# An expert's further passes moved between its base gate/up and down products

## The reference, cut to what matters

```python
logits = (t @ router_w + router_b)           # t: (256, 1024), 32 experts
top_val, top_idx = lax.top_k(logits, 4)      # each token goes to 4 experts
gates = jax.nn.softmax(top_val, axis=-1)
# for every expert e, over the tokens that chose it:
gu = xe @ w_gu[e] + b_gu[e]                  # (n_e, 1024) @ (1024, 2048)
g, u = jnp.split(gu, 2, axis=-1)
g = jnp.minimum(g, 7.0); u = jnp.clip(u, -7.0, 7.0)
act = (u + 1.0) * (g * jax.nn.sigmoid(1.702 * g))
y = (act @ w_down[e] + b_down[e]) * gate     # (n_e, 1024) @ (1024, 1024), summed per token
```

## Time and profile before

| | |
|---|---|
| median of 3 runs | 1359.74 us (1357.9 to 1360.75) |
| the profiled execution: time / span | 1358.61 / 1356.6 us |
| PE, PEld busy | 1284.8 us (95%), 591.3 us (44%) |
| DVE, ACT, POOL busy | 491.4, 187.3, 15.7 us |
| read from memory | 476.1 MB, 352 GB/s over the span |
| chain that ended last | PE 73%, DMA 21%, DVE 3%, issue 2% |

### The profile page before, as it was taken

One profiled execution on the slowest core, in us unless ns is written; L12 is line 12 of the kernel. 1 busy time (PEld: TensorE's weight loads), 2 busy tenths in 40 slices (PEclk: granted clock), 3 DMA queues, 4 the chain that ended last, 5 costly groups with the idle time before them and its releaser, 6 DMA issues.

```text
span 1356.6 us, 16429 instructions
## 1 busy us (share of the span) xinstructions
PE 1284.8 (95%) x5992; PEld 591.3 (44%) x5993; DVE 491.4 (36%) x1030; ACT 187.3 (14%) x377; POOL 15.7 (1%) x48
## 2 busy tenths in 40 slices
PE   4999999999998999999999999999999986999997
PEld 3866866778752333333333333333333321333332
DVE  3032665331143333333333333333333332333334
ACT  2101323332021001000110000110001000001101
POOL 0000000110000000000000000000000000000000
PEclk9999999999999999999999999999999998999999
DMA  9858674326678999999999999999999999399995
GB/s 356 308 186 296 222 241 170 125 73 263 237 289 315 409 428 430 427 430 428 428 429 426 431 427 430 390 427 428 428 429 429 427 430 428 132 431 426 429 428 212
DMA packets 59183, 477.55 MB, mean 352 GB/s; under 512 B 4991, under 2 KB 5076, under 8 KB 32532
## 3 DMA queue, kind: packets, MB, share of 16 engines
q1 hardware_dynamic: 58852, 476.11, 85.6%
q10 hardware_dynamic: 304, 1.06, 0.2%
HBM read 476.10 MB, written 1.05 MB: 352 GB/s over the span
## 4 chain that ended last, share of the span: by engine, by line
PE 73%; DMA 21%; DVE 3%; issue 2%; SPq 0%; ACT 0%; DVEq 0%; ACTq 0%
PE bank L1577 23%; DMA down_ring<-in_w_down 15%; PE bank L1613 14%; PE bank L1260 10%; DMA gu_ring<-in_w_gu 6%; PE bank L1406 4%; PE bank L1253 4%; PE bank L1566 3%; PE bank L1544 3%; PE bank L1308 2%; PE bank L1469 2%; PE bank L1536 1%; PE bank L1367 1%; DVE scratch L1085 1%; DVE scratch L1083 1%
## 5 line engine op out<-in xcount | busy, mean ns | idle before, releaser
L1577 PE MATMUL bank<-gu_ring,scratch 128*64 128x512 f32 x2048 | 464.3, 600 | 12.6 <-issue 7.3
L1577 PEld LDWEIGHTS bank<-gu_ring,scratch 128*64 128x64 f32 x2048 | 143.9, 138 | 299.8 <-issue 292.7
L1613 PE MATMUL bank<-down_ring,scratch 128*64 128x512 f32 x1024 | 233.8, 598 | 18.4 <-DMA down_ring<-in_w_down 13.8
L1260 PE MATMUL bank<-gu_ring 128*128 128x256 f32 x640 | 143.8, 381 | 0.0
L1613 PEld LDWEIGHTS bank<-down_ring,scratch 128*64 128x64 f32 x1024 | 70.1, 136 | 139.2 <-issue 128.9
L1260 PEld LDWEIGHTS bank<-gu_ring 128*128 128x128 f32 x640 | 119.8, 190 | 18.6 <-issue 1.3
L687 ACT ACTIVATE scratch<-bank 128x512 f32<-128x512 f32 x32 | 19.1, 597 | 692.1 <-PE bank L1577 692.1
L1073 DVE TENSOR_TENSOR scratch<-bank,bgu 128x512 f32<-128x512 f32 x32 | 22.2, 692 | 254.5 <-PE bank L1544 254.5
L1055 DVE TENSOR_TENSOR xres<-xres,bank 128x512 f32<-128x512 f32 x132 | 81.8, 682 | 40.1 <-PE bank L1566 40.1
L1544 PEld LDWEIGHTS bank<-ident,scratch 128*128 128x128 f32 x392 | 41.1, 140 | 79.5 <-ACT scratch L687 26.0
L1536 PE MATMUL bank<-xn,onehot 128*64 128x512 f32 x264 | 69.6, 605 | 0.0
(11 more groups left out here) (265 smaller groups left out, 793.3 us busy)
## 6 DMA issues: line engine op xcount, KB each, us to landing
gu_ring<-in_w_gu SPq DMA_DIRECT2D x128, 2048.0 KB, 23.8
down_ring<-in_w_down SPq DMA_DIRECT2D x64, 2048.0 KB, 17.4
gu_ring<-in_w_in SPq DMA_DIRECT2D x32, 1024.0 KB, 7.8
gu_ring<-in_w_ada SPq DMA_DIRECT2D x16, 1024.0 KB, 7.0
down_ring<-in_w_ada SPq DMA_DIRECT2D x8, 512.0 KB, 10.6
gu_ring<-in_w_ada SPq DMA_DIRECT2D x8, 512.0 KB, 11.6
gu_ring<-in_w_pa SPq DMA_DIRECT2D x4, 1024.0 KB, 6.3
gu_ring<-in_w_pb SPq DMA_DIRECT2D x4, 1024.0 KB, 6.3
```

Source lines behind the costliest of these rows:

```text
L1260: last = M(dst[:, b * T:(b + 1) * T], group_chunk(group, kt // 4)[:, kt % 4, cols], hT[:, kt, :], start=kt == 0, stop=kt == KT - 1)
L1577: last = M(bank[f // 2][64 * a:64 * a + 64, :], xT[:, kt % 4, kt // 4, :], gu_ring[:, 8 * half + kt, f * 512:(f + 1) * 512], start=kt == 0 ...
L1613: last = M(bank[7][64 * a:64 * a + 64, :], act_sb[:, kt % 4, kt // 4, :], down_ring[:, kt // 2, (kt % 2) * D + a * 512:(kt % 2) * D + (a + ...
```

## The change

`further_passes` is called in the midst of the expert: on PE behind `way_back` and ahead of base down, on ACT behind `copy_back`, on DVE between the last `act_ready` and `take(item + 1)`. Only the load of the count stays at the expert's head. For this a pass gets small areas of its own: its picks (`f_pick`, `f_gates`), the columns of `u_raw` behind `f_back` (`f_x`), the unused half of `g_sb` (`f_act_sb`), and it gives back through banks 0 to 3 instead of 4 to 7. The picks of an expert's first pass are made for every expert, early in DVE's work (`further_pick`), and those of the next pass in the pass ahead of it. The loop of six turns becomes two by three. PE no longer waits at a pass's end for DVE's adds, nor in a pass for `slot_in`. SP loads from `passes` how many passes stand ahead and waits for `f_gu_done` before it refills a half of the ring.

```diff
-        def further_passes(eng, expert, one_pass):
-            count = eng.value_load(passes[0:1, 0, bass.ds(expert, 1)], min_val=0, max_val=FURTHER_BLOCKS)
+        def further_count(eng, expert):
+            return eng.value_load(passes[0:1, 0, bass.ds(expert, 1)], min_val=0, max_val=FURTHER_BLOCKS)
+        def further_passes(eng, expert, count, one_pass):
             with eng.If(count > 0):
                 before_it = eng.value_load(passes[0:1, 1, bass.ds(expert, 1)], min_val=0, max_val=T * TOPK // FCAP)
-                with eng.Fori(0, FURTHER_BLOCKS) as b:
-                    with eng.If(count > b):
-                        one_pass(b, before_it + b)
+                with eng.Fori(0, 2) as part:
+                    with eng.If(count > part * (FURTHER_BLOCKS // 2)):
+                        with eng.Fori(0, FURTHER_BLOCKS // 2) as n:
+                            b = part * (FURTHER_BLOCKS // 2) + n
+                            with eng.If(count > b):
+                                one_pass(b, before_it + b)
...
             def load_item_gu(item, half):
+                passes_made = sp.value_load(passes[0:1, 2, bass.ds(item - 1, 1)], min_val=1, max_val=T * TOPK // FCAP + 1)
                 for j in range(4):
                     sp.wait_ge(gu_used, item * 8 + (2 * j - 14))
+                    if j == 0:
+                        sp.wait_ge(f_gu_done, passes_made)
...
-            V.tensor_copy(passes[:], passes_f[:]).then_inc(passes_ready, 1)
+            V.tensor_scalar(passes[:, 2, :], passes_f[:, 1, :], 1.0, None, ALU.add)
+            V.tensor_copy(passes[:, 0:2, :], passes_f[:]).then_inc(passes_ready, 1)
...
+            def further_pick(expert, first, made):
+                for tt in range(TT):
+                    V.tensor_scalar(f_pick[:, tt, :], iota[:, 0:FCAP], first,
+                                    r1[:, tt, bass.ds(expert, 1)], ALU.add, ALU.is_equal).then_inc(f_onehot, 1)
+                dve.wait_ge(f_onehot, made * 2 + 2)
+                for tt in range(TT):
+                    V.tensor_scalar(f_gates[:, tt, :, :].rearrange("p a (k s) -> p (a k) s", k=2),
+                                    f_pick[:, tt, :].unsqueeze(1).to_broadcast([P, 4, FCAP]),
+                                    gates[:, tt, bass.ds(expert, 1)], None, ALU.mult).then_inc(f_gated, 1)
...
             def expert(item, half, fills):
+                count = further_count(pe, item)
...
                 way_back(item)
+                further_passes(pe, item, count, lambda b, k: further(item, half, fills, k))
                 for kt in range(KT):
...
             def further(expert, half, fills, k):
-                pe.wait_ge(xTe_ready, expert + 1)
-                pe.wait_ge(back_ready, expert + 1)
-                pe.wait_ge(f_onehot, k * 2 + 2)
+                pe.wait_ge(xraw_ready, expert + 2)
+                pe.wait_ge(f_onehot, (expert + k) * 2 + 2)
...
-                    M(bank[4 + n][:, :], f_back[rows_, tt * P:(tt + 1) * P], f_y[rows_, :], start=True, stop=True
+                    M(bank[n][:, :], f_back[rows_, tt * P:(tt + 1) * P], f_y[rows_, :], start=True, stop=True
                       ).then_inc(f_given, 1)
-                pe.wait_ge(f_added, k * 4 + 4)
-                nc.tensor.transpose(bank[2][:, 0:P], ident[:], ident[:])
```

More of the change, by code:

```diff
@@ L455, in load_item_down @@
                     load_down(item, a)
+            sp.wait_ge(passes_ready, 1)
             load_item_gu(2, 0)
@@ L685, in expert @@
             def expert(item):
+                count = further_count(act, item)
                 act.wait_ge(g_done, item + 1)
@@ L693, in expert @@
                 copy_back(item)
+                further_passes(act, item, count, further)
             def further(b, k):
                 act.wait_ge(f_taken, k + 1)
-                A(in_blocks(x_raw[:, 0:2 * P]), bank[4][:, 0:2 * P].rearrange("s (p r) -> s r p", r=2), ACT.Copy).then_inc(f_xraw, 1)
+                A(in_blocks(f_x), bank[4][:, 0:2 * P].rearrange("s (p r) -> s r p", r=2), ACT.Copy).then_inc(f_xraw, 1)
                 act.wait_ge(f_back_done, k + 1)
                 A(f_back, bank[5][:, 0:T], ACT.Copy).then_inc(f_back_ready, 1)
-                act.wait_ge(f_gu_done, k + 1)
+                act.wait_ge(f_gu_done, k + 2)
                 A(in_blocks(g_raw), by_fours(bank[0][:, :]), ACT.Copy).then_inc(f_raw, 1)
@@ L1004, in _ @@
             dve.wait_ge(counts_done, 1)
-            own.then(V.tensor_scalar(over[:, 0:FURTHER_BLOCKS], pass_start[0:NE, :], bank[0][0:NE, 0:1], None, ALU.is_lt))
+            own.then(V.tensor_scalar(over[:, 0:FURTHER_BLOCKS], pass_start[0:NE, 0:FURTHER_BLOCKS], bank[0][0:NE, 0:1], None, ALU.is_lt))
             V.tensor_reduce(over[:, FURTHER_BLOCKS:FURTHER_BLOCKS + 1], over[:, 0:FURTHER_BLOCKS], AX.X, ALU.add
@@ L1070, in expert @@
                 add_given(item - 1)
+                count = further_count(dve, item)
+                before_it = dve.value_load(passes[0:1, 1, bass.ds(item, 1)], min_val=0, max_val=T * TOPK // FCAP)
+                further_pick(item, pass_start[:, 0:1], item + before_it)
                 dve.wait_ge(gT_done, item + 1)
@@ L1086, in expert @@
                                            ).then_inc(act_ready, 1)
+                further_passes(dve, item, count, lambda b, k: further(item, b, k))
                 take(item + 1)
@@ L1110, in further @@
                 g, u, sg = g_sb[:, :, :, 0:FCAP], u_sb[:, :, :, 0:FCAP], sig[:, :, :, 0:FCAP]
[L1111 to L1119, removed]
+                dve.wait_ge(act_ready, expert * 2 + 2)
                 dve.wait_ge(f_takenT, k + 1)
@@ L1146, in _ @@
             V.memset(small[:, 7:8], 0.0).then_inc(f_mark, 1)
+            V.memset(small[:, 6:7], 0.0).then_inc(f_gu_done, 1)
             with dve.Fori(0, NE) as n:
                 own.start_at(n * PER + start)
-                further_passes(dve, n, lambda b, k: further(n, b, k))
                 expert(n)
@@ L1656, in further @@
                         row = 64 * a + FCAP * (kt % 2)
[L1657 removed]
+                        last = M(bank[7][row:row + FCAP, :], f_act_sb[:, kt % 4, kt // 4, :],
                                  down_ring[:, kt // 2, (kt % 2) * D + a * 512:(kt % 2) * D + (a + 1) * 512],
@@ L1689, in _ @@
                 for half in range(2):
-                    further_passes(pe, n * 2 + half, lambda b, k: further(n * 2 + half, half, n + 1, k))
                     expert(n * 2 + half, half, n + 1)
```

30 lines of the change are left out of this document (16 added, 14 removed).

## The result

| | before | after |
|---|---|---|
| median (range, runs) | 1359.18 us (1357.9 to 1360.75, 4) | 1343.41 us (1342.69 to 1343.86, 4) |
| ratio, 95% interval | | 0.9882 (0.9861 to 0.9903) |
| profiled execution: time / span | 1358.61 / 1356.6 us | 1342.69 / 1340.7 us |
| PE, DVE busy | 1284.8, 491.4 us | 1277.4, 518.2 us |

The kernel is faster by 15.8 us, in the profiled pair by 15.9.

What follows compares the result with a forecast made beforehand. Transfers were taken to bound the experts ahead of the pass (29.37 us), PE those behind (27.37). The sum -11.2 + 0.2 + 0.3 = -10.7 took the profiled 1358.61 to 1347.9 us; median forecast 1349.0, range 1346 to 1352.

Steps and rivals of the forecast that it cites:

- branches in: PE's entry into the pass, a load, three branches and two loop heads: 0.9 us, ends 0.3 and 2.0.
- take to gate/up: Take, copy, transposes and scaling at the pass's start: 3.6 us against 4.1 at half clock, ends 3.2 and 4.1.
- down: The pass's 32 down records on PE, clock partly falling: 5.2 us, ends 3.7 and 6.4.
- result, give back, branches out: End of the pass on PE: 2.6 us for result and give back, 1.5 for branches out.
- the pass: The further pass of expert 25, all exposed in its new place: 25.0 us against 36.2, so -11.2.
- the one-for-one way to the end: Behind the pass PE alone sets the six following experts, so the pass's gain reaches the end undiminished.
- The start: First loop border, where PE stalled 3.49 us: stall may change by -3.5 to +3.5, taken as +0.3.
- The wait for the picks: PE's wait for DVE's picks in the old pass, counted as 2.99 us of the 36.17 the pass adds.
- What every expert pays: PE's branch ahead of base down, DVE's four picks and SP's load, in every expert: 0.
- The first: Deeper gain, clock at its upper level through the pass, branches hidden: -14, 1345.5 us and less; chance 0.10.
- third: Transfers take back what is won: no change, 1359 to 1361 us; chance 0.05.
- The fourth: Slower, the branch in the midst of every expert isn't hidden: 1374 us at 1.5 us each; chance 0.08.

Runs made afterwards that it cites:

- e12: The changed kernel again with no edit, on the same chip as e9 to e11: 1344.08 us, ratio 0.9882.
- e1: The changed kernel with the loop of six turns again in place of two by three: 1346.89 us, ratio 0.9924.
- e2: The changed kernel with every pass's picks made at the head of the pass again, none ahead: 1348.92 us, ratio 0.9933.
- e9: The kernel of e5 with the picks made late, at the head of the pass: 1352.12 us, ratio 0.9943.
- e5: The changed kernel with passes at the expert's head, keeping early picks, small areas, two by three turns, no wait for adds: 1351.94 us, ratio 0.9945.
- e7: The changed kernel with every expert's count of further passes set to 0: 1332.27 us, ratio 0.981.
- e8: The kernel before with every expert's count of further passes set to 0: 1336.67 us, ratio 0.9842.
- e10: The changed kernel with 640 never-reached matmuls behind each pass body on PE, always jumped over: 1651.67 us, ratio 1.2149.
- e11: The changed kernel with 192 never-reached matmuls behind each pass body on PE, always jumped over: 1660.65 us, ratio 1.2215.
- e3: The kernel of e2 with PE also waiting for the pass's adds and a last transpose at the pass's end: 1355.25 us, ratio 0.9972.
- e4: The kernel of e3 with passes back at the expert's head and PE's waits for weights inside the pass: 1357.53 us, ratio 0.9997.
- e6: The kernel before with unused identity products (6, 8, 6 and 8) on PE ahead of the pass's waits: 1359.12 us, ratio 0.9987.

## Why the prediction fell short

The steps, in the order of the prediction, in the profiled pair:

| term, us | predicted | low end | measured |
|---|---|---|---|
| branches in | 0.9 | 0.3 | 0.24 |
| take to gate/up | 3.6 | 3.2 | 3.14 |
| gate/up | 7.15 | | 7.13 |
| middle up to down | 4.04 | | 3.93 |
| down | 5.2 | 3.7 | 3.70 |
| result, give back, branches out | 4.1 | 3.1 | 3.69 |
| the pass | 25.0 | 21.5 | 21.83 |
| ahead of the loop's expert 24 | +0.5 | | -1.6 |

(The pass: 1157.32 less 1106.12, less the period of 29.37.)

- **What bounds, the 29.37 and 27.37 us, one pass at expert 25, the one-for-one way to the end:** right, the periods and the way to the end to 0.1 us.
- **The pass, 3.2 us too long. The failed step is the down product**, "I take 5.2": half of that miss. I let the clock fall because PE stands still about 4 us ahead of it. It does so in some executions (4.96 in e12, 5.06 in e1) and not in others (3.64 in after, and in e2 with the same wait of 2.62). Branches in (0.7 us), the take (0.5) and the way out (0.4) make up the rest. The first two came out just below their low ends (0.24 against 0.3, 3.14 against 3.2): I had bounded the take by the slow old pass, and behind 0.43 us of idle time its 16 records ran at full clock (1.07 us against 1.93), as in e1 and e12. The down product alone did not put the time below the range: in e12 it took 4.96 us, near my 5.2, and that execution took 1344.49 us.
- **The start, 2.1 us off, the largest single term.** This step failed too. I put +0.3 on the stall at the loop's first border (it might double, move or vanish) and +0.2 on DVE's extra instruction. The stall vanished. Of the 1.6 us won there, 1.2 lie ahead of the mixture of experts, in work that the change doesn't touch, and differ between any two executions; 0.4 lie behind, where the mean over the variants is 2.4. Most of the vanished stall is taken back by the transfers later, which the sum should have said: a stall ahead of experts that wait for transfers is not paid one for one. Why the old place fetches at the first border and the new one shows nothing at its jumps isn't settled.
- **The wait for the picks.** I named 2.99 us of "PE's wait for the picks" as part of what the pass cost. The sum didn't use it, but the reason was wrong: e9 against e5 shows that such a wait costs at most 0.6 us there. What made the old pass dear is what came behind the landing at 1128.85: branches that waited for the adds, the clock, and the whole base gate/up.
- **What every expert pays, 0:** right (0.19 us as before, and e7 is not slower than e8). That e7 is 4.4 us faster by the medians is a gain outside the pass that the prediction had no term for and no run explains.
- **The rivals.** The first, "the clock stays at its upper level through the pass, the branches hide", is what the profile shows; I gave it 0.10, against 0.59 for the forecast. The transfers took nothing back (third). The fourth did not occur and would have at a longer jump (e10, e11).

**Where the 16 us come from**, taken apart from the changed kernel by the medians: late picks cost 5.5, the wait for the adds 6.3 more, the old place 2.3 more (not clear of noise, and not in the profiles); six turns by themselves 3.5, of which the profile shows 1.2. Taken away alone, the place costs 8.5. The parts don't add, since in the old place early picks bring next to nothing. By the profile they are 14.35 us at the pass, 13.0 where the clock falls as in e12, and 1.6 at the start. By the medians some 12.6 hang on the pass and up to 4.4 lie outside it (e7, e8). It can't be pinned down further here: the runs of one kernel lie 1.2 us (the four of the changed kernel) to 8 us apart (1355.58 to 1363.5 in 19 runs of the kernel before on one chip). No version that does all the work beat the changed kernel.

## What to carry to other kernels

For optional work in a pipeline with transfers, count in either place what comes behind the last landing it waits for: 3.24 us of wait ahead of it cost at most 0.6 us here (e9), 2.83 us behind it 3.5 to 5.5 (e2). A new place alone may bring nothing, as here while the late picks and the guard stayed (e3, e4). A guard at the end of such work (here PE waiting for DVE's adds) costs its wait and everything queued behind it, so separate areas can be worth more than a better place. Where a term hangs on the clock after a short gap, keep both levels in the range instead of a point between them, and compare profiles of more than one execution.

## What the runs showed of the hardware

- PE's granted clock is not set by the gap ahead alone: behind 2.6 us of idle time ahead of the down product it stayed at 1.00 in two profiles (after, e2) and was at 0.50 for part of the product in three others (e1, e3, e12), of which e12 is the same kernel as after. What decides it is not shown. Filling such gaps with products of the identity moved the low stretches and did not remove them (e6: 1.00 in the take, 0.50 inside the fillers ahead of the down product).
- PE's jumps show no cost up to a point and then a large one: nothing at the pass's body, about 6 us each with 192 matmuls more (e11) and no more than that with 640 (e10); the whole kernel takes 21 to 22% longer. Whether the jump's length or the loop's is the point is open.
